# A context pass moved one round forward, and a new order in a projection stage

## The reference, cut to what matters

```python
for l in range(2):                                   # first block
    x = x + 0.5 * swiglu_ffn(x, ffn1...)             # feed-forwards f = 0, 2
    h = rms_norm(x, mix_norm[l])
    x = x + mixers(h @ w_in[l]) @ w_out[l]           # three attention branches
    x = x + 0.5 * swiglu_ffn(x, ffn2...)             # feed-forwards f = 1, 3

# second block; ctx is a second input of 256 tokens
hc = modulate(rms_norm_2(ctx, g_pre_mix), sm_c, cm_c)
_, _, xs_c, B_c, C_c, dt_c = mixer_inputs(hc, w_in, conv_w, conv_b, 1, ctx_len, False)
_, hf_c, hb_c = ssd_bidir(xs_c, B_c, C_c, dt_c, ...)         # states only
hx = modulate(rms_norm_2(x, g_pre_mix), sm_x, cm_x)
u, z, xs, B, C, dt = mixer_inputs(hx, w_in, conv_w, conv_b, rows, 64, True)
y, _, _ = ssd_bidir(xs, B, C, dt, ..., hf_c, hb_c)
x = x + gm_x * rms_norm_2(mixer_output(u, z, xs, y, ...), g_post_mix)
x = x + gf_x * rms_norm_2(swiglu(modulate(...)), g_post_ffn)  # feed-forward f = 4
```

## Time and profile before

| | |
|---|---|
| median of three runs | 1784.06 us |
| the profiled execution | 1790.11 us |
| its span | 1788.2 us |
| mean granted TensorE clock | 0.976 |
| busy: PE, DVE, ACT, POOL | 94%, 68%, 51%, 12% |
| chain that ended last: PE, DVE, ACT | 84%, 10%, 4% |

### The profile page before, as it was taken

The page is one execution under the profiler, slowest core; times in us unless marked ns, Lnnn a source line. Parts: engine busy times, 40 slices in busy tenths (PEclk is TensorE's granted clock), DMA queues, the critical chain, the costliest instruction groups (busy, mean ns, idle before and its releaser), DMA issues.

```text
span 1788.2 us, 30567 instructions
## 1 busy us (share of the span) xinstructions
PE 1689.2 (94%) x13524; PEld 1602.8 (90%) x13524; DVE 1215.5 (68%) x1377; ACT 909.7 (51%) x1078; POOL 214.0 (12%) x124
## 2 busy tenths in 40 slices
PE   5999999999999999999999999989999879879997
PEld 5999987899999999999987899989999859769997
DVE  5655677677776557766677668766897586476654
ACT  4444555684444445544554675455556456244542
POOL 0000000000120000100000000141224346600000
PEclk9999999999999999999999999999999879989999
DMA  6567643444556665566653444455555223225551
GB/s 233 209 222 263 227 179 141 153 142 152 189 215 214 244 227 189 213 236 239 229 184 141 142 142 165 166 188 188 189 187 189 95 71 119 95 71 189 189 189 48
DMA packets 45491, 315.53 MB, mean 176 GB/s; under 512 B 5296, under 2 KB 6064, under 8 KB 7728
## 3 DMA queue, kind: packets, MB, share of 16 engines
q1 hardware_dynamic: 44496, 312.78, 48.5%
q10 hardware_dynamic: 864, 0.80, 0.1%
HBM read 312.51 MB, written 1.05 MB: 175 GB/s over the span
## 4 chain that ended last, share of the span: by engine, by line
PE 84%; DVE 10%; ACT 4%; issue 1%; POOL 1%; DMA 0%; ACTq 0%; DVEq 0%
PE ps L1070 23%; PE ps L1071 22%; PE ps L1072 22%; PE ps L1246 3%; PE ps L1248 3%; PE ps L1247 3%; DVE wlo L1645 2%; PE ps L1050 1%; DVE pre L2204 1%; PE ps L1260 1%; PE ps L1438 1%; ACT whi L590 1%; PE ps L1271 1%; DVE dA_rows L1645 1%; PE ps L1497 1%
## 5 line engine op out<-in xcount | busy, mean ns | idle before, releaser
L590 ACT ACTIVATE whi<-raw 128x2048 fp32r<-128x2048 f32 x267 | 506.7, 1910 | 330.3 <-DMA raw<-in_w_dram 330.1
L1645 DVE TENSOR_TENSOR wlo<-raw,whi 128x2048 fp32r<-128x2048 f32 x245 | 566.7, 2321 | 119.6 <-ACT whi L590 117.0
L1070 PE MATMUL ps<-h1hi,whi 128*128 128x256 f32 x1792 | 505.5, 282 | 17.2 <-DVE wlo L1645 17.2
L1071 PE MATMUL ps<-h1hi,wlo 128*128 128x256 f32 x1792 | 500.2, 279 | 0.0
L1072 PE MATMUL ps<-h1lo,whi 128*128 128x256 f32 x1792 | 500.1, 279 | 0.0
L1070 PEld LDWEIGHTS ps<-h1hi,whi 128*128 128x128 f32 x1792 | 340.1, 190 | 28.7 <-issue 28.1
L1072 PEld LDWEIGHTS ps<-h1lo,whi 128*128 128x128 f32 x1792 | 338.3, 189 | 0.0
L1071 PEld LDWEIGHTS ps<-h1hi,wlo 128*128 128x128 f32 x1792 | 337.9, 189 | 0.1
L1070 PE MATMUL ps<-hid_hi,whi 128*128 128x256 f32 x880 | 250.3, 284 | 13.7 <-DVE hid_lo L1645 13.7
L1071 PE MATMUL ps<-hid_hi,wlo 128*128 128x256 f32 x880 | 246.9, 281 | 0.0
L1072 PE MATMUL ps<-hid_lo,whi 128*128 128x256 f32 x880 | 246.8, 280 | 0.0
(11 more groups left out here) (320 smaller groups left out, 2508.2 us busy)
## 6 DMA issues: line engine op xcount, KB each, us to landing
raw<-in_w_dram SPq DMA_DIRECT2D x291, 1024.0 KB, 4.8
relbias<-in_relbias_dram SPq DMA_DIRECT2D x2, 1024.0 KB, 6.9
pv<-in_pv_dram SPq DMA_DIRECT2D x2, 641.0 KB, 6.0
xT<-in_x_dram SPq DMA_DIRECT2D x4, 256.0 KB, 4.1
ctxT<-in_ctx_dram SPq DMA_DIRECT2D x1, 1024.0 KB, 6.8
out_dram<-xT SPq DMA_DIRECT2D x4, 256.0 KB, 2.5
decay<-in_decay_dram ACTq DMA_DIRECT2D x1, 512.0 KB, 16.2
dft_tok<-in_dft_tok_dram SPq DMA_DIRECT2D x1, 512.0 KB, 5.6
```

Source lines behind the costliest of these rows:

```text
L590: act.activation(whi[:, slot, :], raw[:, slot, :], ACT.Copy).then_inc(hi_done[slot], 1)
L1070: pe.matmul(out, w_hi, hi, start=start, stop=False, skip_group_check=skip)
L1071: pe.matmul(out, w_lo, hi, start=False, stop=False, skip_group_check=skip)
L1645: return dve.tensor_tensor(out, a, b, op)
```

## The change

`ctx_of` places the context slabs in rounds 1 to 6. All steps of the context pass move one round forward with them, on TensorE, ScalarE and VectorE; ScalarE's copy of CTX0 now stands between two slabs ahead of the feed-forward. `dt_value(0)` also moves from the middle of its round to the end. `hidden_hi` moves ahead of `ctx_tokens`. TensorE's wait for `ctok_ready` ahead of the states goes.

In the projection stage ScalarE takes a chunk from its bank first and does the other work (w1, u_t, the exponentials, tokens) behind it. The second transform step and the sums stand one chunk earlier on TensorE, the segment steps behind chunks 10 to 15 in place of 9, 10, 11, 13, 14, 15. On VectorE `dt_value(1)` stands ahead of the first convolution, and the two `dA_rows` behind convolutions 4 and 9 in place of 3 and 8.

```diff
--- before.py
+++ after.py
@@ -78,3 +78,3 @@

-    return i - 2 if f == 3 and 2 <= i <= N_CTX + 1 else None
+    return i - 1 if f == 3 and 1 <= i <= N_CTX else None

@@ -649,4 +649,4 @@
                 bank = 6 - 2 * (i % 2)
-                if ctx_of(f, i + 1) is not None:
-                    cut_hi(CTX0 + ctx_of(f, i + 1))
+                if i < N_CTX:
+                    cut_hi(CTX0 + i)
                 j = ctx_of(f, i)
@@ -661,11 +661,11 @@
                     act.activation(aexp, vec2("a_log"), ACT.Exp).then_inc(a_exp, 1)
+                if i == 3:
+                    softplus_exp(0)
                 if i == 4:
-                    softplus_exp(0)
-                if i == 5:
                     softplus_ln(0)
-                if 0 <= i - 4 < N_CTX:
-                    j = i - 4
+                if 0 <= i - 3 < N_CTX:
+                    j = i - 3
                     act.wait_ge(cconv_low, j + 1)
                     sigmoid(ccex[:, j % 2, ctx_half(j)]).then_inc(cconv_sig, 1)
-                if i == 8:
+                if i == 7:
                     act.wait_ge(csums_done, 1)
@@ -676,3 +676,3 @@
                 bank = 6 - 2 * (i % 2)
-                j = i - 5
+                j = i - 4
                 if not 0 <= j < N_CTX:
@@ -709,5 +709,5 @@
                 cut_hi(g0 + 3 * i + 3)
+                hidden_hi(i)
                 if f == 3:
                     ctx_tokens(i)
-                hidden_hi(i)
                 cut_hi(g0 + 3 * i + 4)
@@ -888,2 +888,4 @@
             cut_hi(m + 2)
+            if l == DEPTH - 1:
+                cut_hi(CTX0)
             cut_hi(m + 3)
@@ -960,15 +962,2 @@
         for c, (kind, j) in enumerate(ORDER):
-            if c == 6:
-                act.wait_ge(dft1_done, 1)
-                act.activation(w1[:, :, :], ps_flat[:, 2048:3072], ACT.Copy).then_inc(w1_ready, 1)
-            if c == 8:
-                act.wait_ge(dft2_done, 1)
-                act.activation(u_t[:, :, :], ps[:, 6, :], ACT.Copy).then_inc(dft_ready, 1)
-            if c == 9:
-                act.wait_ge(sums_done, 1)
-                act.activation(tail_x, ps[:, 7, 128:224], ACT.Exp).then_inc(tail_ready, 1)
-            if c in (9, 11, 13, 16, 18):
-                tokens((9, 11, 13, 16, 18).index(c))
-            if c in (10, 11, 12, 14, 15, 16):
-                seg_exps((10, 11, 12, 14, 15, 16).index(c))
             if kind == "dt":
@@ -978,8 +967,6 @@
                 conv_base(j)
+                if j == 1:
+                    softplus_ln(1)
                 if j >= 1:
                     conv_sigmoid(j - 1)
-                if j == 1:
-                    softplus_exp(1)
-                if j == 2:
-                    softplus_ln(1)
             else:
@@ -990,2 +977,17 @@
                 cut_hi(b2 + c // 2 + 4)
+            if c == 3:
+                softplus_exp(1)
+            if c == 6:
+                act.wait_ge(dft1_done, 1)
+                act.activation(w1[:, :, :], ps_flat[:, 2048:3072], ACT.Copy).then_inc(w1_ready, 1)
+            if c == 7:
+                act.wait_ge(sums_done, 1)
+                act.activation(tail_x, ps[:, 7, 128:224], ACT.Exp).then_inc(tail_ready, 1)
+            if c == 8:
+                act.wait_ge(dft2_done, 1)
+                act.activation(u_t[:, :, :], ps[:, 6, :], ACT.Copy).then_inc(dft_ready, 1)
+            if 11 <= c <= 16:
+                seg_exps(c - 11)
+            if c in (9, 11, 13, 16, 18):
+                tokens((9, 11, 13, 16, 18).index(c))
             if c == 19:
@@ -1138,3 +1140,3 @@
                 bank = 6 - 2 * (i % 2)
-                if i == 3:
+                if i == 2:
                     pe.wait_ge(cpre_evac, 2)
@@ -1144,6 +1146,6 @@
                     ins.then_inc(cdt_done, 1)
-                j = i - 5
+                j = i - 4
                 if 0 <= j < N_CTX:
-                    pe.wait_ge(cpre_evac, min(i - 1, N_CTX))
-                    if i == 8:
+                    pe.wait_ge(cpre_evac, min(i, N_CTX))
+                    if i == 7:
                         pe.wait_ge(tail_ready, 1)
@@ -1162,7 +1164,7 @@
                 if ctx_of(f, i) is not None:
-                    pe.wait_ge(cpre_evac, i - 1)
-                if i == 3:
+                    pe.wait_ge(cpre_evac, i)
+                if i == 2:
                     pe.wait_ge(dt_abs, 1)
-                if 5 <= i < 5 + N_CTX:
-                    pe.wait_ge(ctok_ready, i - 4)
+                if 4 <= i < 4 + N_CTX:
+                    pe.wait_ge(ctok_ready, i - 3)

@@ -1452,3 +1454,2 @@
         pe.wait_ge(hid_ready, 2 * DEPTH * FI)
-        pe.wait_ge(ctok_ready, N_CTX)
         pe.wait_ge(xw_ready, 1)
@@ -1531,8 +1532,8 @@
                 ins.then_inc(sums_done, 1)
+            if 10 <= c <= 15:
+                if c == 10:
+                    pe.wait_ge(masks_ready, 1)
+                segments(c - 10)
             if c in (8, 10, 12, 15, 17):
                 tokens((8, 10, 12, 15, 17).index(c))
-            if c in (9, 10, 11, 13, 14, 15):
-                if c == 9:
-                    pe.wait_ge(masks_ready, 1)
-                segments((9, 10, 11, 13, 14, 15).index(c))
             if c == 5:
@@ -1545,3 +1546,3 @@
                 ins.then_inc(dft1_done, 1)
-            if c == 7:
+            if c == 6:
                 pe.wait_ge(w1_ready, 1)
@@ -1803,8 +1804,5 @@
                 cut_lo(g0 + 3 * i + 2)
-                if f == 3 and 0 <= i - 3 < N_CTX:
-                    ctx_conv(i - 3, 0)
+                if f == 3 and 0 <= i - 2 < N_CTX:
+                    ctx_conv(i - 2, 0)
                 up(i)
-                if f == 3 and i == 3:
-                    dve.wait_ge(cdt_done, 1)
-                    dt_value(0, ps[:, 4, 0:48])
                 if ada_of(f, i) is not None:
@@ -1817,4 +1815,4 @@
                     cut_lo(g0 + 3 * i + 3)
-                if f == 3 and 0 <= i - 3 < N_CTX:
-                    ctx_conv(i - 3, 1)
+                if f == 3 and 0 <= i - 2 < N_CTX:
+                    ctx_conv(i - 2, 1)
                 cut_lo(g0 + 3 * i + 4)
@@ -1831,7 +1829,10 @@
                     ins.then_inc(cmod_ready, 1)
+                if f == 3 and i == 2:
+                    dve.wait_ge(cdt_done, 1)
+                    dt_value(0, ps[:, 6, 0:48])
+                if f == 3 and i == 3:
+                    dt_plus(0)
                 if f == 3 and i == 4:
-                    dt_plus(0)
-                if f == 3 and i == 5:
                     dt_final(0)
-                if f == 3 and i == 8:
+                if f == 3 and i == 7:
                     dve.wait_ge(tail_ready, 1)
@@ -2217,2 +2218,4 @@

+        dve.wait_ge(dt_tok_done, 1)
+        dt_value(1, ps[:, 7, 0:48])
         for j in range(NCONV):
@@ -2220,11 +2223,8 @@
             if j == 0:
-                dve.wait_ge(dt_tok_done, 1)
-                dt_value(1, ps[:, 7, 0:48])
+                dt_plus(1)
             if j == 1:
-                dt_plus(1)
-            if j == 2:
                 dt_final(1)
                 dve.wait_ge(dA_ready, 2)
-            if j in (3, 8):
-                tt = int(j == 8)
+            if j in (4, 9):
+                tt = int(j == 9)
                 at_least(dve, seg_done, 3 * tt)
```

## The result

| | before | after |
|---|---|---|
| median, same chip | 1787.09 us (1781.81 to 1792.11) | 1832.3 us (1829.62 to 1833.77) |
| the profiled execution | 1790.11 us | 1837.69 us |
| its span | 1788.2 us | 1835.8 us |
| mean granted clock | 0.976 | 0.969 |

A forecast was written before the change was run, and what follows sets the result against it. TensorE, busy 94% of the span, was taken as the bound. Waits and restarts of 17.9 + 28.1 = 46.0 us on the profiled 1790.1 us gave 1836.1, or 1830 on the median; range 1804 to 1846.

The forecast's parts named there:

- stretch one: Last feed-forward of layer 2 with the context pass, 1163 to 1379 us; predicted to lose 17.9 us.
- stretch two: Projection stage of the second block, 1392 to 1505 us; predicted to lose 28.1 us.
- Two of the signs: Changed profile, 1400 to 1520 us: more slices with clock digit below 9; longest segment wait 8 to 10 us, on `dA_rows`.
- The context product: Feed-forward 3, round 1: TensorE stands 16.6 us until 1186.5 for the split of CTX0, in place of 5.9; loss 10.7 us.
- `dt_value(0)`: Context pass, end of round 2 on VectorE: TensorE stands 5.0 us (3.5 to 5.5) before round 3, plus 2.2 us restart.
- The tokens: Context pass: the 1.2 us wait only moves to round 7; the place behind `hidden_hi` takes away waits nobody has.
- The projection stage: Second block: TensorE's waits add up to 34.1 us against 14.8, +19.3; with restarts 28.1 us.
- The restarts: TensorE's low clock after each wait over 2 us: 2.2 us each; four more in the projection stage, 8.8 us.
- Only stretch one: Rival: the projection stage loses nothing, as earlier bases and early `dA` pay for the serial segments; 1802 us; chance 0.10.
- Stretch two worse: Rival: in the projection stage TensorE restarts low for the chunks between waits too; +13 us, 1843; chance 0.15.
- Faster because the context product fills the idle time: Rival: context product runs in the idle time at the first down product; 1755 us; chance 0.02.
- No change: Rival: both stretches hide their waits, so no change that can be told, about 9 us; chance 0.03.

The follow-up runs named there:

- experiment 7: Changed kernel with 36 dummy TensorE products ahead of the wait for `hlo`, one execution; stretch one 230.15 us, context product 5.69 us instead of 7.01.
- experiment 2: Kernel before with the projection stage's edits only, context pass as before; 1814.0 us, ratio 1.0162 to the kernel before.
- experiment 9: Changed kernel with the second `dA_rows` behind convolution 8 in place of 9; 1826.5 us, ratio 1.0241 to the kernel before.
- experiment 10: Changed kernel with `dt_value(1)` behind the first convolution again; 1830.1 us, ratio 1.0271 to the kernel before.
- experiment 3: Changed kernel with ScalarE making the context's high part `hhi` ahead of its wait for the variance; 1816.7 us, ratio 1.0176 to the kernel before.
- experiment 1: Kernel before with the context pass edits only, projection stage as before; 1802.3 us, ratio 1.0098 to the kernel before.
- experiment 8: Changed kernel with ScalarE's segment exponentials ahead of the chunk's base again; 1812.8 us, ratio 1.0169 to the kernel before.
- experiment 11: Changed kernel with the w1 copy ahead of the base of convolution 3 again, one execution; stretch two 6.2 us shorter.
- experiment 6: Changed kernel with `dt_value(0)` back right behind the hidden tile and tokens ahead of `hidden_hi`, `hhi` left late; 1826.1 us, ratio 1.0238 to the kernel before.

## Why the prediction was right

Forecast 1830 us, range 1804 to 1846; measured 1832.3. It was right for its reasons: each wait that it named is there, at its engine. That the two stretches came out within 0.8 us of the forecast is partly luck. Other traces of the same program text put stretch one 15.2 to 18.8 us above the kernel before, and the terms of stretch two miss by up to 1.8 us each, some up and some down. Two of the signs did not come: the page has no more slices with a clock digit below 9 between 1400 and 1520 than before (two in each; the new one lies at 1150 to 1190), and the longest segment wait is 7.5 us, not 8 to 10. The terms, one by one.

**The context product.** Predicted 16.6 us of idleness until 1186.5; measured 15.94, until 1186.38. GpSimd in the changed kernel:

```profile
1174.01 6.98 POOL L523 TENSOR_TENSOR hlo<-ctxT,hhi 128x512 fp32r<-128x512 f32 x4 [17.45 <-ACT hhi L696]
1180.95 5.28 POOL L487 TENSOR_TENSOR wlo<-raw,whi 128x1024 fp32r<-128x1024 f32 x2
```

The split of CTX0 took 5.28 us, between the 4.70 alone and the 6.82 of the earlier trace rows. The reading by which VectorE's whole split would be added (1187.8) was too high by 1.4 us here.

**`dt_value(0)`.** Predicted 5.0 us, measured 4.74. VectorE in round 2:

```profile
1225.17 3.08 DVE L1763 SCALAR_TENSOR_TENSOR cpost<-cpre,pc,cpost 128x253 f32<-128x253 f32 x6
...
1228.50 2.28 DVE L1646 TENSOR_TENSOR wlo<-raw,whi 128x2048 fp32r<-128x2048 f32 x1
1230.70 0.20 DVE L1646 TENSOR_TENSOR small<-ps,pc 128x48 f32<-128x48 f32 x1
1230.93 0.21 DVE L1727 SCALAR_TENSOR_TENSOR small<-small 128x48 f32<-128x48 f32 x1
```

This is the list that the order of instructions showed: a convolution, a split, and behind them 0.4 us of work for which TensorE waits. The transposes for dt came at 1220.5, so nearly all the delay is the queue.

**The tokens.** Here the prediction was wrong. It said that the 1.2 us wait only moves to round 7 and that the place behind `hidden_hi` takes away "waits that nobody has". Instead a wait of 1.8 us for `cxs_tok` came. ScalarE:

```profile
1320.29 0.63 ACT L641 ACTIVATE hid_hi<-t_hid 128x512 fp32r<-128x512 f32 x1 [2.90 <-DVE t_hid L1646]
1320.83 0.64 ACT L686 ACTIVATE cxs_tok<-ps 128x256 f32<-128x256 f32 x2
```

The copy stands behind `hidden_hi` now, and that waits for VectorE's hidden tile. With its restart this is 3.6 us, in place of the 1.2 us that the sum carried over. In the total it is partly offset: the first wait and the wait for `dt_value` were 0.9 us shorter than booked together, and the first restart cost 1.4 us, not 2.2.

**The projection stage**, waits in us:

| TensorE waits for | predicted | measured |
|---|---|---|
| `pre`, chunk 5 | 3.7 | 4.0 |
| `w`, second transform | 4.7 | 4.9 |
| `u_t` | 2.4 | 3.6 |
| `xs_tok` | 0 | 1.2 |
| `seg`, segments 1, 2, 4, 5 | 4.8, 1.5, 2.9, 4.8 | 5.9, 1.5, 2.8, 4.6 |
| `dA_rows`, segment 3 | 9.3 | 7.5 |

The largest miss is segment 3. VectorE:

```profile
1499.82 0.29 DVE L2211 TENSOR_SCALAR cex<-pre 128x256 f32<-128x256 f32 x1
1500.03 3.42 DVE L1646 TENSOR_TENSOR dA_rows<-tri,small 128x1536 f32<-128x1536 f32 x2
```

The two row products took 3.42 us, less than either end of the earlier trace rows (4.48 and 6.17), and GpSimd has no instruction beside them here. The first two of the same kernel, and GpSimd beside them:

```profile
1459.24 6.11 DVE L1646 TENSOR_TENSOR dA_rows<-tri,small 128x1536 f32<-128x1536 f32 x2
1456.80 4.72 POOL L487 TENSOR_TENSOR wlo<-raw,whi 128x1024 fp32r<-128x1024 f32 x2 [1.06 <-ACT whi L590]
```

Both rows of before were disturbed ones in this way (GpSimd splits slabs from 1434.74 and from 1458.63), and the trace of before held no undisturbed one. The wait for `u_t` has 1.0 of its 1.2 us more from the same split: VectorE's clamp beside it took 2.50 us from 1456.82, where it takes 0.29 us alone, and the sigmoid ahead of the copy waits 1.02 us for it. Segment 1 came 1.1 us above its list. ScalarE:

```profile
1475.80 0.56 ACT L933 ACTIVATE pre<-ps,pc 128x256 f32<-128x256 f32 x1 [1.89 <-PE ps L1074]
1477.56 0.42 ACT L606 ACTIVATE cex<-cex 128x256 f32<-128x256 f32 x1 [1.20 <-DVE cex L2211]
...
1478.78 1.89 ACT L590 ACTIVATE whi<-raw 128x2048 fp32r<-128x2048 f32 x1
1480.58 1.06 ACT L958 ACTIVATE seg<-ps 128x512 f32<-128x512 f32 x2
```

The durations are those of the earlier trace rows, but the sigmoid in the middle of the list waits 1.20 us for VectorE's clamp: a list behind a chunk can hold a wait of its own.

**The restarts.** 2.2 us for each wait over 2 us, less those of before: 2.2 net in stretch one and 8.8 in stretch two. The excess of a block over its undisturbed length was 1.4, 2.7 and 1.8 us in stretch one, and the wait of 1.8 us, which also had one, lies below the bound of 2 us that I set. In stretch two the excess behind the seven waits over 2 us is 1.7 to 3.1 us, 2.1 in the mean (each run of products up to the next wait, against the fastest passes of the same products in the traces with the same TensorE program). Less those of before it is 7.7 us, against 8.8. Single sizes were wrong, the term was right, and experiment 7 shows what it is: filled with products, the same wait leaves no low clock. A second way to it, an estimate from the two traces: TensorE is busy for 57 us at 1.2 GHz before and for 76 us now, and at half the clock half of that is lost, 28 and 38 us, so 10 us more. The Trainium skill, "TensorE: Matmul & The Clock Gate", "What's actually happening", says that the ramp is under 1% of a typical span and need not be fitted, and would leave the term out. The trace does not agree: by the estimate above the low clock costs 38 us, 2.1% of the span, and the restarts that came made some 11 of the 47 us by which the stretches grew.

**The rivals.** Only stretch one: fell by experiment 2. Stretch two worse, with TensorE low throughout (+13 us): fell, its clock is back in the block behind each wait. Faster because the context product fills the idle time: fell; even with `hhi` early its gain went to the norm. No change: fell.

## What to carry to other kernels

In an in-order list, price a moved instruction by what now stands ahead of it on its engine, waits included, and count from the moment at which the product that releases it ends; here 0.4 us of work behind a convolution and a split cost 4.7 us, and 1 us of exponentials behind a base, a sigmoid and a copy cost up to 5.9 us at each step. A wait that is taken away shows only what was late next, so repair all links of a chain before you judge one: experiments 9 and 10 gave back 2.0 and -0.35 us alone. Before an engine is given work earlier, look at what it runs beside: GpSimd's early split cost VectorE's norm 5 us.

## What the runs showed of the hardware

VectorE's small operations take six to eight times as long beside a GpSimd split (2.51 us in place of 0.42, 2.31 in place of 0.29, experiment 3), and its row products 6.11 us in place of 3.42. The convolutions on `pre`, which read their chunk from the PSUM bank, keep their time: in the kernel before one starts at 1435.84, wholly beside a GpSimd split of 5.75 us that starts at 1434.74, and takes 3.02 us, as the others do (3.02 to 3.04).

At a granted clock of 1.00 a chunk of 48 products takes two different times. Windows of TensorE in the kernel before:

```profile
1210.90:1216.34 5.44, 5.44 (x50) 1.00 0.60 193
1244.61:1250.26 5.65, 5.65 (x50) 1.00 0.52 186
```

The products start 0.113 us apart in one and 0.118 us apart in the other. The slower pace begins right behind small transposes (1227 us) and ends at the next ones (1273 us). After a wait in this part of the program it is the faster pace in the changed kernel and in experiments 1, 3, 7, 8, 9 and 11, but not in experiment 10, where the slower one goes on behind a wait of 4.6 us. In experiment 6, which has no wait there, the slower one held for seven chunks, 1.5 us. Over all of the rest it makes some 274.5 us in some executions and some 281.4 us in others, which is most of the spread between executions. Its cause stays open. It is also why the lengths of the stretches, and the waits in them, decide the small differences here, and not the times.

What a restart costs isn't constant, even for the same wait in the same program text. The context product behind the 15.9 us takes from 7.01 us (changed kernel) to 8.2 us (experiment 11), against 5.69 us filled. The restart behind the wait of 4.7 us costs about 2.7 us in the changed kernel and in experiments 1 and 8, and 1.4 to 1.7 us in experiments 3, 7, 9, 10 and 11; that behind the wait of 1.8 us (1.3 us in experiment 10) costs 1.8 us in the first three and 0.1 to 0.3 us in the others. After the 1.2 us wait of the earlier trace rows there is none. This, more than the waits, is the scatter of S1.
